# The filter stage of a hybrid diffusion step, with its modulation blocks, output pairs and folds in another order

## The reference, cut to what matters

```python
def _modulation(cond, w_mod, b_mod):
    m = jax.nn.silu(cond.astype(F32)) @ w_mod.astype(F32) + b_mod.astype(F32)
    return jnp.split(m[:, None, :], N_MOD, axis=-1)

def _hyena_filters(L, w1, b1, w2, b2, w3, freq):
    ...
    h = (hid @ w3.astype(F32)).reshape(L, 2, HY_ORDER, HY_W)
    ...
    h = h * jnp.exp(-t[:, :, None, None] * jnp.abs(deltas))
    h = h / jnp.sum(jnp.abs(h), axis=(0, 1), keepdims=True)
    fwd, bwd = h[:, 0], h[:, 1]
    circ_filter = jnp.concatenate([fwd, jnp.zeros_like(fwd[:1]), bwd[:0:-1]], axis=0)
    return jnp.fft.rfft(circ_filter, axis=0)

def _trunk_layer(x, cond, p, layer_idx, ctx_k, ctx_v, s0):
    sh1, sc1, g1, sh2, sc2, g2 = _modulation(cond, p['w_mod'], p['b_mod'])
    h = _rmsnorm(x, p['norm_g'][0]) * (1.0 + sc1) + sh1
    z = jnp.einsum('bld,de->ble', h, p['w_in'].astype(F32))
    ...
```

## Time and profile before

| | us |
|---|---|
| Median of 3 runs | 4164.59 (4164.25 to 4165.73) |
| Profiled execution, its run | 4167.97 |
| Profiled execution, its span | 4166.1 |
| TensorE busy in the span | 3785.1 (91%) |
| Filter stage of layer 0, from its first send to the next stage's first matmul | 4.93 to 140.94 |
| Filter stage of layer 1 | 2069.36 to 2204.88 |

### The profile page before, as it was taken

How to read it: one execution, slowest core, us unless ns; L and a number is a source line. 1 busy time by engine, 2 the same in 40 slices (tenths; PEclk the granted TensorE clock), 3 DMA queues, 4 the chain that set the end, 5 groups by cost and what they waited for, 6 DMA issues and landing times. The chain is left out here.

```text
span 4166.1 us, 55492 instructions
## 1 busy us (share of the span) xinstructions
PE 3785.1 (91%) x23454; PEld 3035.9 (73%) x23454; DVE 1623.6 (39%) x2886; ACT 1139.1 (27%) x2898; POOL 178.2 (4%) x110
## 2 busy tenths in 40 slices
PE   8899998986949999999889999989869499999996
PEld 3477875665429999999735688656654299999995
DVE  4248723877351111111151577248773511111112
ACT  3442212873111111111145222148721111111112
POOL 0000001000000000000000000110000000000000
PEclk9899999998979999999999999999989799999998
DMA  7311021011346877777582111210112477788784
GB/s 284 144 45 47 29 79 70 1 51 56 108 167 210 281 280 281 267 268 269 177 304 81 48 44 39 76 60 1 66 66 103 157 258 267 265 281 281 266 281 173
DMA packets 319422, 648.97 MB, mean 156 GB/s; under 512 B 19838, under 2 KB 57342, under 8 KB 318408
## 3 DMA queue, kind: packets, MB, share of 16 engines
q1 hardware_dynamic: 305640, 596.14, 39.5%
q0 software_dynamic: 9216, 33.56, 3.5%
q10 hardware_dynamic: 4320, 15.73, 1.0%
HBM read 581.41 MB, written 63.98 MB: 155 GB/s over the span
## 5 line engine op out<-in xcount | busy, mean ns | idle before, releaser
L2123 PE MATMUL ps<-arena 128*128 128x144 f32 x8192 | 1014.9, 287 | 10.3 <-DVE arena L2283 10.3
L2123 PEld LDWEIGHTS ps<-arena 128*128 128x128 f32 x8192 | 1008.0, 190 | 17.9 <-DVE arena L2283 17.9
L291 PE MATMUL ps<-arena 128*128 128x384 f32 x1920 | 627.9, 488 | 3.9 <-PEq L89 3.9
L291 PEld LDWEIGHTS ps<-arena 128*128 128x128 f32 x1920 | 363.9, 191 | 251.4 <-issue 6.7
L2147 PE MATMUL ps<-arena 128*128 128x144 f32 x4096 | 507.1, 286 | 0.0
L2147 PEld LDWEIGHTS ps<-arena 128*128 128x128 f32 x4096 | 503.6, 190 | 0.0
L2294 DVE TENSOR_TENSOR arena<-arena,ps 128x144 f32<-128x144 f32 x256 | 77.8, 304 | 920.1 <-ACT arena L2199 920.1
L2199 ACT ACTIVATE arena<-ps 128x144 f32<-128x144 f32 x256 | 74.5, 291 | 1011.4 <-PE ps L2123 1011.4
L433 ACT ACTIVATE arena<-ps 128x384 f32<-128x384 f32 (+1 forms) x192 | 86.2, 449 | 693.4 <-PE ps L291 461.1
L288 PE MATMUL ps<-arena 128*128 128x256 f32 x1152 | 257.5, 381 | 0.0
L2283 DVE TENSOR_SCALAR arena<-ps,mod 128x128 f32<-128x128 f32 x256 | 87.1, 403 | 435.5 <-PE ps L2103 435.5
(11 more groups left out here) (323 smaller groups left out, 3508.9 us busy)
## 6 DMA issues: line engine op xcount, KB each, us to landing
arena<-in_w_gate SPq DMA_DIRECT2D x64, 2048.0 KB, 7.9
arena<-in_w_up SPq DMA_DIRECT2D x64, 2048.0 KB, 14.1
arena<-in_w_down SPq DMA_DIRECT2D x64, 2048.0 KB, 12.4
arena<-in_w_mod SPq DMA_DIRECT2D x24, 2048.0 KB, 15.5
arena<-in_w_in SPq DMA_DIRECT2D x28, 1024.0 KB, 5.2
arena<-in_dft_units SPq DMA_DIRECT2D x26, 512.0 KB, 7.3
arena<-x_rows SPq DMA_DIRECT2D x23, 512.0 KB, 6.1
x_rows<-arena ACTq DMA_DIRECT2D x18, 512.0 KB, 2.6
```

The lines of the kernel that those rows point to most:

```text
L291: last = nc.tensor.matmul(m.ps[:, at:at + TC], m.Wr[:, slot % 2, k, jj * P:(jj + 1) * P], m.hT[:, k, q * TC:(q + 1) * TC], start=(k == 0), ...
L2123: last = nc.tensor.matmul(m.ps[:, at:at + CAP], m.wbuf[:, 2 * h + which, k, q * P:(q + 1) * P], m.xe[:, e % 2, k, :], start=(k == 0), stop ...
```

## The change

The order is another; no arithmetic of the result is left out.

- `PAIRS` goes by halves of the frequencies: both parts of half 0 come first, then those of half 1. Fold 0 now stands behind pair 4, fold 1 behind pair 8.
- Blocks 3 to 9 now lie among the output pairs, one behind each of six pairs and one behind the gate rows; 10 follows the context pair and 11 the column sums.
- `rows` is split in `gate` (behind modulation 5, with PSUM banks of its own, which the tiles' turning uses afterwards) and `sum` (last of all).
- The fold works in place in steps that each wait for the one before (`fold_step`). Its eight results are eight separate views, so SyncE stores them in 16 pieces of 256 KB and not in four of 1 MB.
- The late pair of the real part is written where the magnitudes lay, and waits for the last sum of them.
- SyncE sends the modulation blocks 10 and 11 both behind the stores of fold 0, and each of the next weight blocks as soon as the token tile in its place is turned.

```diff
+PAIRS = [("late", 1, 0), ("early", 1, 0), ("late", 0, 0), ("gate", 0, 0), ("early", 0, 0),
+         ("late", 1, 1), ("early", 1, 1), ("late", 0, 1), ("early", 0, 1), ("ctx", 0, 0), ("sum", 0, 0)]
...
             for ft in range(2):
+                sp.wait_ge(s["folded"], ft + 1)
                 for part in range(2):
-                    sp.wait_ge(s["folded"], 2 * ft + part + 1)
-                    sp.dma_start(f[:, part, ft], m.folded[ft][part]).then_inc(s["stored"], 16)
-                load_w(10 + ft)
+                    for g in range(4):
+                        sp.dma_start(f[:, part, g, ft], m.folded[ft][part][g]).then_inc(s["stored"], 16)
+                if ft == 0:
+                    load_w(10)
+                    load_w(11)
...
-            sp.wait_ge(s["transposed"], 2 * NT)
             for b in range(2):
+                sp.wait_ge(s["transposed"], 2 * (NT - 1 + b))
                 sp.dma_start(m.Wr[:, b], w_in_block(m, l, b)).then_inc(s["next_w"], 16)
...
             def turn_x(t):
                 pe.wait_ge(s["row_normed"], t + 1)
+                if t == 0:
+                    wait_taken(pe, GATE)
...
                 if kind == "late":
                     act.wait_ge(s["spectrum"], q + 1)
-                    if part == 0:
-                        act.wait_ge(s["absolute"], NT)
+                    if part == 0 and ft == 0:
+                        act.wait_ge(s["added"], LT - 1)
...
             def fold(ft):
 
-                dve.wait_ge(s["spectrum"], LAST_LAT + 1)
-                wait_taken(dve, LAST_LAT)
-                if ft:
-                    dve.wait_ge(s["folded"], 2)
+                wait_taken(dve, LAST_OF[ft])
                 (er, gr, fr, kr), (ei, gi, fi, ki) = ([m.parts[part][ft][n // 2][:, n % 2] for n in range(4)] for part in range(2))
-                out = m.folded[ft]
-                nc.vector.tensor_tensor(out[0][:, 0], er, gr, ALU.add)
-                nc.vector.tensor_tensor(out[0][:, 1], er, gr, ALU.subtract)
...
+                free = m.spare[ft]
+                for x, y in ((er, gr), (ei, gi), (fr, ki), (fi, kr)):
+                    steps.then_wait(dve, nc.vector.tensor_tensor(free, x, y, ALU.subtract))
+                    steps.then_wait(dve, nc.vector.tensor_tensor(x, x, y, ALU.add))
+                    free = y
+                dve.sem_inc(s["folded"], 1)
```

More of the change, by code:

```diff
@@ L944 @@
 PI_BELOW = 3.1415925
-PAIRS = [("late", 1, 0), ("early", 1, 0), ("late", 1, 1), ("early", 1, 1),
-         ("late", 0, 0), ("early", 0, 0), ("late", 0, 1), ("early", 0, 1), ("rows", 0, 0), ("ctx", 0, 0)]
-TAKERS = {"late": ("act",), "early": ("act", "dve"), "ctx": ("act",), "rows": ("dve",)}
+PAIRS = [("late", 1, 0), ("early", 1, 0), ("late", 0, 0), ("gate", 0, 0), ("early", 0, 0),
+         ("late", 1, 1), ("early", 1, 1), ("late", 0, 1), ("early", 0, 1), ("ctx", 0, 0), ("sum", 0, 0)]
+TAKERS = {"late": ("act",), "early": ("act", "dve"), "ctx": ("act",), "gate": ("dve",), "sum": ("dve",)}
 TAP_PAIRS = ((4,), (0, 5), (1, 6), (2, 7), (3, 8))
 MAG_ORDER = [0, 8, 4, 5, 6, 7, 1, 2, 3]
[L952 to L957, removed]
+AFTER = {0: [("abs", 4), ("abs", 5), ("abs", 6), ("mod", 3)],
+         1: [("edge", 0), ("abs", 7), ("abs", 1), ("abs", 2), ("abs", 3), ("mod", 4)],
+         2: [("norm", 0), ("mod", 5)],
+         3: [("norm", 1), ("x", 0), ("mod", 6)],
+         4: [("norm", 2), ("x", 1), ("fold", 0), ("mod", 7)],
+         5: [("x", 2), ("norm", 3), ("mod", 8)],
+         6: [("norm", 4), ("x", 3)],
+         7: [("norm", 5), ("x", 4), ("mod", 9)],
+         8: [("x", 5), ("norm", 6), ("fold", 1)],
+         9: [("norm", 7), ("x", 6), ("mod", 10)],
+         10: [("norm", 8), ("x", 7), ("mod", 11), ("x", 8), ("turn", 11)]}
 def mag_slot(i):
@@ L978, in modulate_filter_norm, with banks @@
     GATE_BLOCKS = (4, 5)
-    ROWS_PAIR = PAIRS.index(("rows", 0, 0))
-    LAST_LAT = ROWS_PAIR - 1
+    GATE = PAIRS.index(("gate", 0, 0))
+    LAST_OF = [PAIRS.index(("early", 0, ft)) for ft in range(2)]
+    def banks(q):
+        n = q - (q > GATE)
+        return 2048 if q == GATE else (n % 2) * 1024
     TURNED = {b: i + 1 for i, b in enumerate(x for x in range(HB) if x not in GATE_BLOCKS)}
@@ L1130, in _ @@
             for q, (kind, part, ft) in enumerate(PAIRS):
+                base = banks(q)
                 if q < 2:
                     pe.wait_ge(s["taps"], 2 * len(TAP_PAIRS))
-                else:
-                    wait_taken(pe, q - 2)
-                base = (q % 2) * 1024
-                if part == 0 and kind != "rows":
+                elif q != GATE:
+                    wait_taken(pe, max(i for i in range(q) if i != GATE and banks(i) == base))
+                if kind in ("late", "early") and part == 0 or kind == "ctx":
                     pe.wait_ge(s["edge_rows"], 1)
@@ L1142, in _ @@
                                                 m.fu[:, n, LT, :], start=True, stop=True)
-                elif kind == "rows":
+                elif kind == "gate":
                     pe.wait_ge(s["rows_kept"], GATE_BLOCKS[-1] + 1)
@@ L1406, in _ @@
                     take_early(q, part, ft)
-                elif kind == "rows":
-                    take_rows(q)
+                elif kind == "gate":
+                    take_gate(q)
+                elif kind == "sum":
+                    take_sum(q)
                 if q == 0:
@@ L2497, in build @@
         m.parts = [[[view(at, 2, 512) for at in both] for both in part] for part in
[L2498 to L2499 removed]
+                   (((35072, 36096), (21248, 23296)), ((25856, 26880), (27904, 28928)))]
+        m.spare = [view(at, 512) for at in (15360, 15872)]
+        m.folded = []
+        for ft in range(2):
+            (er, gr, fr, kr), (ei, gi, fi, ki) = ([m.parts[part][ft][n // 2][:, n % 2] for n in range(4)] for part in range(2))
+            m.folded.append([[er, m.spare[ft], gi, fr], [ei, gr, fi, ki]])
         m.f_ctx = view(29952, 2, 512)
```

39 lines of the change are left out of this document (18 added, 21 removed).

## The result

The changed kernel takes 4173.44 us (median of 15 runs, 4171.29 to 4179.19), the kernel before 4166.10 in the same session (15 runs, 4164.25 to 4169.77). The ratio is 1.0019, 95% interval 1.0011 to 1.0027: 7.3 us slower, which lies inside the 0.2% that was to count as no change, but clear of zero. The forecast of +2.4 us had the sign and not the size.

The account below looks back on a forecast made before the run. TensorE was taken to bound the filter stage's first part, a chain between engines ending at the next weights' landing the second. Layer 0 -0.8 + 0.5, layer 1 +1.0 + 1.7: +2.4 us on 4164.59, forecast 4167, range 4154 to 4177.

Parts of the forecast that it names:

- 6.4 + 9.1 = 15.5: Filter stage's end, behind fold 1: 6.4 us for the stores' bytes, then 9.1 for the next stage's two weight blocks.
- The other way to the end: Filter stage's end through tiles 7 and 8 and the second weight block's landing: 139.2, against 139.5 through SyncE's queue.
- Turn 7: Block 7's turn waits for a VectorE reduction behind all of fold 0: TensorE idle 1.1 us.
- The small stores: Fold 1's eight 256 KB stores stream like large ones; rival, done in turn: +17 us per layer, 4201, chance 0.04.
- The projection of layer 1: Next stage's 288 matmuls in layer 1 take 94.8 us after TensorE idles some 5 us: +1.7 us.
- the bounds of 137 and 143: Layer 0's filter stage, forecast to end near 139.5; the prediction is wrong if it ends before 137 or after 143.
- The gate rows' gap: TensorE idles 3.5 us ahead of the gate rows, waiting for ScalarE's copy of block 5, held by the last magnitude sum.
- The edge rows' wait: In the dense part, pair 2 waits for edge rows made by VectorE: 1.1 us of new idle TensorE.
- The clock: One half-clock spell behind the gate rows' gap: gate rows +0.9, tile +0.85, part of modulation 6 +1.4, 3.2 us.
- the rival in which the clock falls more often: Two more half-clock spells of 2.3 us ahead of fold 1 in each layer: 4176, chance 0.13.
- the clock staying up: Rival: full clock at the gate rows, 3.2 us less ahead of pair 8 in each layer: 4161, chance 0.28.
- The projection of layer 0: Next stage's 288 matmuls in layer 0, 94.81 us before from a low clock: up to +0.5 us.

Follow-up runs that it names:

- the first experiment: The changed kernel with the gate rows one output pair later and modulation 6 ahead of the first token tile: 4157.68 us, ratio 0.9982 to the kernel before.

## Why the prediction was right, and where its sizes were off

The mechanism held: TensorE's new gaps push fold 1, fold 1 its stores, and they and tile 8 together the next stage. The fold in place took 0.72 us a step and eight made 5.8. The end of the stage lay 15.8 and 15.2 us behind fold 1's first store, for 6.4 + 9.1 = 15.5 in the sum. In layer 0 the first weight block was sent 6.5 us behind that store and the last wait ended 9.3 later. The sum had the 6.4 as the time of the bytes, with 5 us of sends hidden under them; the eleven sends took 6.5 us, so which of the two makes this term is not separated. The other way to the end, by tile 8, came out near to it, as the sum had it (0.3 us apart there; 1.3 and 0.1 by the run with the stores sent early). Turn 7 waited 1.14 for 1.1, the first tile 1.64 for 1.6. The small stores streamed, at 383 GB/s. The projection of layer 1 took 94.78 for 94.8. The stage ended at 142.8, or 141.2 without the 1.6 us by which its first pair had begun late, for 139.5. As measured it lies inside the bounds of 137 and 143 by only 0.2 us. The whole, 4173.44, lies in the upper part of the range of 4154 to 4177; it was the range that caught it, and not the forecast of 4167.

The terms of the sum that were mis-sized, in layer 0:

- **The gate rows' gap: 4.36 us, not 3.5.** I had counted the four sums on GpSimd from 56.4 at 1.26 us each. Two of them took 3.06 together, not 2.5, and ahead of each of the last two GpSimd stood idle for 0.63 us, waiting for its maximum, so that the last ended at 65.7; less the 1.6 of the late start that is 64.1, for 62.8. The run without the wait for that sum shows its price: 2.06 us of the gap.
- **The edge rows' wait** was 1.14 in all, split 0.46 + 0.68, for 1.1: right.
- **The clock: more spells than the one I priced.** The first cost 0.93 + 0.90 + 1.23 = 3.1 us, for 3.2. Then, behind 1.94 us of idleness and tile 6, modulation 10 took 3.16 us, and tile 7 ran at half clock. These lie behind pair 8 and did not move fold 1, as the rival in which the clock falls more often would have it. For the clock staying up the prediction named one gap of 3.47 us; the trace of before has three of 3.47, and behind the other two (129.06 and 2183.96) the tile ran at 1.94 us.
- **The units.** Without gaps and clock the work from the first pair to pair 8's end took 63.6 us, for 62.7 in the sum.
- Together, less the 1.6: pair 8's end at 114.9 for 113.2, fold 1 at 125.3 for 123.8.
- **The projection of layer 0: +1.4 us, not up to +0.5.** I had taken 94.81 as the price of a cold start and thought that layer 0 had paid it already. Behind 7.46 us of idleness it took 96.18, so it can cost nearly twice as much. The idle time alone doesn't tell: behind 7.38 us (the run without the sum's wait) it took 94.83.

Layer 1 lost 1.5 for 1.0 in the stage and 1.7 for 1.7 behind it. The sum of the parts is then +0.8 + 1.5 + 1.4 + 1.7 = 5.4 against my +2.4; the other 1.9 of the 7.3 us I cannot place in the change, and of the last 1.7 only 0.2 shows in the length of its stage. The late start of layer 0 (1.6 us) is a clock spell ahead of every changed instruction, and whether the change makes it likelier is open: in the runs above the first pair of layer 0 began anywhere between 40.2 and 41.75.

**Where the expected gain went.** The change spreads modulation blocks over the pairs, where before six of them lay in the tail with gaps between them. TensorE is now busy for 7 us more behind 101 us, since the last pairs fall there. But how full TensorE is there does not end the stage; the last landing does. In the kernel before, fold 1's stores went out under the loads of blocks 10 and 11; now they stand directly ahead of the next stage's weights. And the gate rows, brought forward beside a chain over VectorE, GpSimd and ScalarE, opened gaps in the one part that TensorE bounded. Undoing that one placement gives 15 us (ratio 1.0019 to 0.9982). In layer 0 the gaps ahead of pair 8's end shrink from 8.3 to 3.2 us and 3.1 us of half clock go, 8.2 in all, and all of it arrives at the end, because fold 1 and tile 8 both follow pair 8. With the gate rows there, the rest of the change is a gain over the kernel before (0.9982, 0.9973 to 0.9991).

The Trainium skill ("TensorE: Matmul & The Clock Gate", "What's actually happening") calls the clock's window free-running. The runs agree, in that the same gaps kept the clock in one place and lost it in another. Behind gaps of 0.27 and 1.76 us the second tile ran at 1.06 us in both layers of the first experiment, and at 1.94 in layer 0 of the run that sends each store when it is ready. A single gap of 3.43 kept the clock and one of 1.90 did not. No run here tells in advance which will.

**Left open.** The end of the stage is a near tie between SyncE's queue and the tiles, and no run parts them cleanly. The in-place fold and the order of pairs by halves were never run apart from the placement of the modulation blocks. The gap between the runs with and without the six unused matmuls is within their intervals.

## What to carry to other kernels

Read a stage from its end: here the last landing in SyncE's queue decided. What stands ahead of it in the queue, and what it waits for itself (here tile 8), counts more than how full the busiest engine is. When an operation is moved into a part that an engine fills completely, look up how many engines its input passes through, since each hand-over and each buffer that it shares with another chain becomes idle time there. Send each piece of a result as soon as it is made, if the queue that carries it also carries what the next stage waits for; here that was run only together with tile 8's move, and gained in one layer of the two.

## What was not expected of the hardware

- A float32 matmul of 128x512 runs as two instructions of 0.43 to 0.44 us, 0.875 us together; a filler that is sized by one of them is twice too long.
- Half clock in the tail of the kernel before (0.70 on average over 40 us) could be filled away without any gain in the whole (1.0002, 0.9993 to 1.0011, with the clock at 0.95 in that stretch): layer 0's stage was 1.9 us shorter, the rest took it back.
- An idle TensorE can charge the next stage too, and not by the length of its idleness: the same 288 matmuls took 93.12 us behind 0.42, 1.15, 2.55 and 3.43 us of it, 94.8 behind 1.07, 1.31, 1.90, 5.20 and 7.38, and 96.18 behind 7.46. The charge arrives on average only: over all 13 profiled executions shown here the seven projection stages with 93.12 took 552.2 to 555.1 us, mean 553.4, and the other nineteen 553.8 to 556.8, mean 555.0.
- Two weight blocks of 1 MB sent together landed 8.8 to 9.3 us after the first send in the kernel before, where the stores had long been sent (10.2 in layer 0 of its run with fillers). With 2.6 MB of stores sent just ahead of them the whole took 15.8 us, 6.5 more; 2.6 MB at the 383 GB/s of that stretch would be 6.8 us, an estimate.
